# A hybrid decoder layer on one core: the order of the seven block products, accumulating DMAs in place of loads and adds, and stores in two halves

## What is computed

```python
g_gdn, g_moba = split(h @ w_in[:, gates])                 # 2 x 2048 columns
y_gdn, y_moba = oa @ w_out_gdn, ob @ w_out_moba           # 1024 -> 2048 each
merged = sigmoid(g_gdn) * y_gdn + sigmoid(g_moba) * y_moba
x = x + merged @ w_o                                      # 2048 -> 2048
```

## Time and profile before

| | |
|---|---|
| median of 3 runs | 1692.65 us |
| the profiled execution, its own time | 1691.26 us |
| its span, first to last instruction | 1689.6 us |
| granted TensorE clock, mean | 0.987 |
| busy: PE, PEld, DVE, ACT, POOL | 95%, 79%, 67%, 46%, 7% |
| HBM read, written | 199.42 MB, 25.17 MB |
| DMA share, mean rate | 38.4% (SP's queue) and 3.8% (POOL's), 133 GB/s |

### The profile page before, as it was taken

The page is one execution under the profiler, slowest core; times in us unless marked ns, Lnnn a source line. Parts: engine busy times, 40 slices in busy tenths (PEclk is TensorE's granted clock), DMA queues, the critical chain, the costliest instruction groups (busy, mean ns, idle before and its releaser), DMA issues.

```text
span 1689.6 us, 20990 instructions
## 1 busy us (share of the span) xinstructions
PE 1613.4 (95%) x7913; PEld 1332.7 (79%) x7913; DVE 1139.4 (67%) x1367; ACT 780.6 (46%) x1032; POOL 110.3 (7%) x111
## 2 busy tenths in 40 slices
PE   6999999999999999999999998999999887997997
PEld 6888888888888888888888876888888666775786
DVE  5745646646546457456478669687788977798975
ACT  5434434434345344344344344656567544454432
POOL 4100001000001010000011000000000000000000
PEclk9999999999999999999999999999999988999999
DMA  8214222323132142142234264736657466764651
GB/s 253 76 30 127 56 76 81 81 74 87 50 83 79 48 106 81 27 128 56 74 106 131 98 230 145 261 126 223 195 186 244 165 216 215 249 235 151 219 203 64
DMA packets 203644, 225.32 MB, mean 133 GB/s; under 512 B 8035, under 2 KB 140358, under 8 KB 202054
## 3 DMA queue, kind: packets, MB, share of 16 engines
q1 hardware_dynamic: 197126, 199.44, 38.4%
q0 software_dynamic: 6464, 25.17, 3.8%
HBM read 199.42 MB, written 25.17 MB: 133 GB/s over the span
## 4 chain that ended last, share of the span: by engine, by line
PE 82%; DVE 8%; DMA 4%; issue 3%; ACT 2%; SPq 0%; POOL 0%; DVEq 0%; ACTq 0%; POOLq 0%
PE bank L643 14%; PE bank L647 14%; PE bank L645 14%; PE bank L1063 8%; PE bank L1065 8%; PE bank L1067 8%; PE bank L672 6%; DVE ring_lo L1974 2%; PE bank L677 1%; ACT ring_hi L1408 1%; DMA operands<-in_w_in_dram 1%; PE bank L834 1%; DVE e_block L1994 1%; DMA branch_a<-e_block 1%; PE bank L850 1%
## 5 line engine op out<-in xcount | busy, mean ns | idle before, releaser
L643 PE MATMUL bank<-h_hi_r,w_hi 128*128 128x512 f32 x1008 | 421.4, 418 | 0.0
L647 PE MATMUL bank<-h_hi_r,w_raw_r 128*128 128x512 f32 x1008 | 396.8, 394 | 0.0
L645 PE MATMUL bank<-h_lo_r,w_hi 128*128 128x512 f32 x1008 | 394.2, 391 | 0.0
L1408 ACT ACTIVATE ring_hi<-operands 128x1024 fp32r<-128x1024 f32 x224 | 234.6, 1058 | 248.8 <-PE bank L1067 179.6
L1974 DVE TENSOR_TENSOR ring_lo<-operands,ring_hi 128x1024 fp32r<-128x1024 f32 x224 | 271.9, 1221 | 105.0 <-ACT ring_hi L1408 104.2
L647 PEld LDWEIGHTS bank<-h_hi_r,w_raw_r 128*128 128x128 f32 x1008 | 189.1, 188 | 42.9
L645 PEld LDWEIGHTS bank<-h_lo_r,w_hi 128*128 128x128 f32 x1008 | 190.2, 189 | 35.6 <-issue 1.7
L643 PEld LDWEIGHTS bank<-h_hi_r,w_hi 128*128 128x128 f32 x1008 | 190.0, 188 | 35.8 <-issue 1.7
L1063 PE MATMUL bank<-ring_hi,h_hi_r 128*128 128x512 f32 x480 | 192.0, 400 | 13.6 <-DVE ring_lo L1974 6.9
L1065 PE MATMUL bank<-ring_lo,h_hi_r 128*128 128x512 f32 x480 | 190.0, 396 | 0.0
L1539 DVE TENSOR_TENSOR w_raw_r<-w_raw,w_hi 128x2048 fp32r<-128x2048 f32 x64 | 146.7, 2292 | 46.3 <-ACT w_hi L1121 45.1
(11 more groups left out here) (308 smaller groups left out, 2154.1 us busy)
## 6 DMA issues: line engine op xcount, KB each, us to landing
w_raw<-in_w_in_dram SPq DMA_DIRECT2D x64, 1024.0 KB, 6.0
operands<-in_w_in_dram SPq DMA_DIRECT2D x96, 512.0 KB, 5.0
operands<-in_w_o_dram SPq DMA_DIRECT2D x48, 512.0 KB, 6.7
operands<-in_w_out_gdn_dram SPq DMA_DIRECT2D x24, 512.0 KB, 5.0
operands<-in_w_out_moba_dram SPq DMA_DIRECT2D x24, 512.0 KB, 5.8
gates<-e_block POOLq DMA_DIRECT2D x16, 512.0 KB, 5.0
operands<-gates SPq DMA_DIRECT2D x16, 512.0 KB, 6.1
x_tiles<-in_x_dram SPq DMA_DIRECT2D x4, 1024.0 KB, 10.4
```

The source lines that it names most:

```text
L643: pe.matmul(PJ[slot % 2][:], w_hi[slot % 2][:, c], h_hi[:, k, :], start=(k == 0), stop=False, skip_group_check=True)
L645: pe.matmul(PJ[slot % 2][:], w_hi[slot % 2][:, c], h_lo[:, k, :], start=False, stop=False, skip_group_check=True)
L647: mm = pe.matmul(PJ[slot % 2][:], w_lo[slot][:, c], h_hi[:, k, :], start=False, stop=(k == KT - 1), skip_group_check=True)
L1408: act.activation(ring_hi[:, n % RINGS, :], ops[:, SOURCE[p], j, :], ACT.Copy).then_inc(s["op_hi"], 1)
```

## The change

The product order of quads 1 to 9 becomes P11, PS1, PS2, P12, PS4, PS3, P22; quad 0 keeps its order. The roles of the four weight blocks change with it (some sums have the other sign, and the token rows of the stage behind quads 6 and 7 are exchanged), and slots are used otherwise: A holds 11, then T1, then T2; B holds 12, then T3; C holds 21, then T4. In the quads of 4 pieces, T2 = T1 + 22 is made by a DMA on POOL's queue that adds 22 from HBM onto the piece in SBUF, and VectorE makes three sums for each piece; 22 is also loaded plainly once for PS4. In the quads of 2 pieces 22 has two places of its own (A2, A3), each block is loaded once, and VectorE makes four sums. In quads 4 to 7 a fourth `e_block` lies over a free piece of B. The addition of `branch_a` in quads 6 and 7 is an accumulating DMA of POOL, each issued after the one before has landed. The result is filled with x by one 4 MB DMA from HBM to HBM in quad 1, the running values of quads 8 and 9 are copied out by ScalarE, and each result block is added onto the result by two accumulating DMAs of 256 KB. `merged_turn` moves from two to four units after the product's end, `merged_copy` (ACT) from six to eight.

```diff
+FIRST_ORDER = (P11, P12, PS1, PS2, PS4, PS3, P22)
+ORDER = (P11, PS1, PS2, P12, PS4, PS3, P22)
...
+def e_index(q, role):
+    if q < Y0:
+        return (0, 1, 2, 0)[role]
+    return (3, 1, 2, 0)[role] if q < W0 else (2, 1, 0, 2)[role]
...
+TURN, CAUGHT_UP = 4, 8
...
+            return {P11: SLOT_A, PS1: SLOT_A, PS2: SLOT_A, P12: SLOT_C, PS4: SLOT_A, PS3: SLOT_B, P22: SLOT_C}[p], j
...
+            def load_22(q):
 
                 for j in range(ku(q)):
...
+                    if ku(q) == 4:
+                        sp.wait_ge(s["op_lo"], unit(q, PS2, j) + 1)
+                        sp.wait_ge(s["t_formed"], t4_formed(q, j))
+                        load_op(q, SLOT_A, j, 1, 1, j)
                     else:
...
+                        last = 2 + j if ku(q - 1) == 4 else j
+                        sp.wait_ge(s["op_lo"], unit(q - 1, PS4, last) + 1)
+                        sp.wait_ge(s["t_formed"], t3_formed(q - 1, last))
+                        load_op(q, SLOT_A, 2 + j, 1, 1, j)
...
+                if q == 1:
+                    sp.dma_start(outs, xs).then_inc(s["out_filled"], 16)
...
-            load_first(0)
-            load_third(0)
+            load_11(0)
+            load_21(0)
+            load_12(0, range(4))
             sp.wait_ge(s["o_out"], 16 * H)
             load_own(0, sums32(0), s["stage_a"])
-            load_second(0)
...
+            def add_22(q, j):
+
+                pool.wait_ge(s["op_lo"], unit(q, PS1, j) + 1)
+                pool.dma_start(ops[:, SLOT_A, j, :].rearrange("p (k c) -> p k c", k=UK), right(q, 1, 1, j),
+                               accum_op=ALU.add).then_inc(acc[j], 16)
...
+                elif q < W0:
+                    b = 4 * (q - YB) + i
+                    g, k = gate_block(q, i)
+                    pool.wait_ge(s["y_g"], 8 + b + 1)
+                    pool.wait_ge(e_stored[k], stored(q - 2))
+                    if b > 0:
+                        pool.wait_ge(s["part_added"], 16 * b)
+                    pool.dma_start(e, m_dram[q - YB, k], accum_op=ALU.add).then_inc(s["part_added"], 16)
+                else:
+                    pool.wait_ge(s["out_filled"], 16)
+                    for t in range(2):
+                        pool.wait_ge(s["c_add"], 2 * (4 * q + i) + 1 + t)
+                        pool.dma_start(token_block(outs, q, i)[:, t, :], block(q, i)[:, t, :], accum_op=ALU.add)\
+                            .then_inc(e_stored[i], 16)
 
             for q in range(NQ):
...
+                if q == W0:
+                    finish_block(q - 1, 3)
+                if ku(q) == 4:
+                    add_22(q, 0)
+                    add_22(q, 1)
+                if q > 0 and q != W0:
+                    finish_block(q - 1, 3)
+                if ku(q) == 4:
+                    add_22(q, 2)
+                    add_22(q, 3)
+                for i in range(3):
+                    finish_block(q, i)
...
+            def forms(q, n):
+
+                at = n - unit(q)
+                if ku(q) == 4:
+                    late = 1 if q == W0 else 0
+                    if q > 0 and late <= at < 4 + late:
+                        form_t1(q, at - late)
+                    elif 12 <= at < 16:
+                        form_t4(q, at - 12)
+                    elif 17 <= at < 21:
+                        form_t3(q, at - 17)
+                elif at < 2:
+                    form_t1(q, at)
+                elif at < 4:
+                    form_t2(q, at - 2)
+                elif 6 <= at < 8:
+                    form_t4(q, at - 6)
+                elif 8 <= at < 10:
+                    form_t3(q, at - 8)
```

More of the change, by code:

```diff
@@ L638, in _ @@
+            for i in range(4):
+                pool.wait_ge(e_stored[i], stored(NQ - 1))
+        @program.tensor
         def _(pe):
@@ L1403, in op_hi @@
                     act.wait_ge(s["pe_unit"], n - LEAD + 1)
-                if p in (P11, P12, PS4):
-                    act.wait_ge(op_loaded[SOURCE[p]][j], op_loads(q, j, SOURCE[p], (P11, P12, PS4).index(p) // 2))
-                else:
-                    act.wait_ge(s["t_formed"], formed(q, (PS1, PS2, PS3, P22).index(p), j))
-                act.activation(ring_hi[:, n % RINGS, :], ops[:, SOURCE[p], j, :], ACT.Copy).then_inc(s["op_hi"], 1)
+                slot, u = source(q, p, j)
+                if p == P11 or p == P12 or (p == PS4 and ku(q) == 2):
+                    act.wait_ge(op_loaded[slot][u], op_loads(q, u, slot))
+                elif p == PS4:
+                    act.wait_ge(op_loaded[slot][u], op_loads(q, u, slot, 1))
+                elif p == PS1:
+                    act.wait_ge(s["t_formed"], t1_formed(q, j))
+                elif p == PS2 and ku(q) == 4:
+                    act.wait_ge(acc[j], added(q))
+                elif p == PS2:
+                    act.wait_ge(s["t_formed"], t2_formed(q, j))
+                else:
+                    act.wait_ge(s["t_formed"], (t3_formed if p == PS3 else t4_formed)(q, j))
@@ L1507, in _ @@
             copy_out(0, P11)
-            merged_hi_at = {unit(W0 - 1, P12, 1): P11, unit(W0, P11, 3): P12, unit(W0, P12, 2): PS1,
-                            unit(W0, PS1, 2): PS2, unit(W0, PS2, 1): PS4, unit(W0, PS2, 3): PS3,
-                            unit(W0, PS4, 1): P22}
+            merged_hi_at = {unit(W0 - 1, PS4, 1): P11, unit(W0, PS1, 1): PS1, unit(W0, PS2, 0): PS2,
+                            unit(W0, PS2, 1): P12, unit(W0, P12, 0): PS4, unit(W0, P12, 1): PS3,
+                            unit(W0, P12, 3): P22}
             for n in range(8, N_UNITS):
                 op_hi(n)
-                for q in range(W0):
+                for q in range(NQ):
                     for p in (P11, PS1, PS2, PS3):
@@ L1531, in _ @@
                     merged_hi(merged_hi_at[n])
-        @block.vector
+        @program.vector
         def _(dve):
@@ L1973, in op_lo @@
                     dve.wait_ge(s["o_mm"], 4 * H)
[L1974 removed]
+                dve.tensor_tensor(ring_lo[:, n % RINGS, :], operand(q, p, j),
                                   ring_hi[:, n % RINGS, :].bitcast(F32), ALU.subtract).then_inc(s["op_lo"], 1)
             head(last, last - 1)
[L1979 to L1986 removed]
             def block_add(q, i):
[L1990 removed]
+                e, p = block(q, i), BLOCK_PRODUCT[i]
                 dve.wait_ge(s["pe_unit"], ended(q, p))
@@ new lines, in form_t2, with form_t4 @@
+                dve.tensor_tensor(ops[:, SLOT_A, j, :], ops[:, SLOT_A, j, :], ops[:, SLOT_A, 2 + j, :], ALU.add)\
+                    .then_inc(s["t_formed"], 1)
+            def form_t4(q, j):
+                if ku(q) == 4:
+                    dve.wait_ge(acc[j], added(q))
+                else:
+                    dve.wait_ge(s["t_formed"], t2_formed(q, j))
+                dve.wait_ge(s["op_hi"], unit(q, P12, j) + 1)
+                dve.tensor_tensor(ops[:, SLOT_C, j, :], ops[:, SLOT_C, j, :], ops[:, SLOT_A, j, :], ALU.subtract)\
@@ L2156, in _ @@
                 for qb in range(NQ):
-                    for pb in range(NP):
-                        if n == ended(qb, pb) + LEAD - 1:
-                            if qb >= W0 and pb in (P11, PS1, PS2, PS3):
-                                residual(qb, pb)
-                            if pb in BLOCK_PRODUCT:
-                                block_add(qb, BLOCK_PRODUCT.index(pb))
-                forms(q, p, j)
+                    for i in range(4):
+                        if n == ended(qb, BLOCK_PRODUCT[i]) + LEAD - 1:
+                            block_add(qb, i)
+                forms(q, n)
                 if q == 0:
```

469 lines of the change are left out of this document (223 added, 246 removed).

## The result

The changed kernel takes 1649.0 us (median of 4 runs, 1646.6 to 1651.3), the kernel before 1691.7 in the same session: a ratio of 0.9748, 95% interval 0.9731 to 0.9765. The forecast was 1650.

What follows compares the result with a forecast made beforehand. TensorE sets the end; its pauses, 87.6 us, are the pool. 10 + 14.8 + 13.5 + 10 - 4 - 1.3 = 43.0 us off 1691.3 gives 1648.3, median said as 1650; range 1634 to 1684, forecast's own 1638 to 1662.

Steps and rivals of the forecast that it cites:

- Quad 0: Two VectorE load waits and four sums go, two T1 passes lie uncovered: 10 of 20.1 us gained, ends 4.9 and 16.2.
- Quads 4 and 5: Late loads and store waits go, VectorE's work stays: 14.8 us gained, ends 4 and 20.
- the three causes: In quads 4 and 5: late loads of 11, P12 waiting for the previous quad's block_add, the copy after P11 waiting for a store.
- Quads 6 and 7: VectorE falls under 38.3 us in both; 2.6 and 5.5 us stay lost: 13.5 us gained if the new DMA comes in time.
- The charge for the turns: Accumulating DMAs of branch_a take 6 to 7 us from issue to landing; 0.5 us charged at each of 8 turns: minus 4.
- Rival 3: Added DMA late for the turns, 12 us with the wait for the one before: 26 us less gain, 1676 us; chance 0.12.
- Quad 8: VectorE falls to 78.4 us, PS1's left operand is ready 5 us late: 10 us gained, ends 2 and 15.
- T2: T2's additions by DMA land in 7 us, inside the 14.3 us available less the issue: cost 0.
- Rival 1: Accumulating DMAs slow in the engines, above 5 us each TensorE waits in six quads; at 8.0, 1721 us; chance 0.12.
- The 4 MB copy: HBM copy in quad 1 takes at least 11 us, SP's next loads queue behind it: cost 0, up to 5 at half rate.
- The end: The last result block's two accumulating halves land later: +1.3 us, ends -0.3 and +5.
- the forecast's own signs: Quads 0, 4, 5, 6, 7, 8 about 87, 47, 40, 41, 44, 87 us; T2 landing 6 to 7; transpose waits under 1.

Runs made afterwards that it cites:

- the plain DMAs: Against the changed kernel with one semaphore per block for the branch_a additions: T2's additions as plain loads, the result's half blocks as plain stores; 1640.2 us.
- the old order: Against the changed kernel: old order of products in quads 1, 2 and 9, the previous quad's last block stored ahead of the first additions; 1646.1 us.
- three moves: Against the changed kernel with one semaphore per block for the branch_a additions: three instructions moved up in quads 4 and 8; 1639.2 us.

## Why the prediction was right, step by step

- **Quad 0** (10 forecast, 10.2 measured). The upper end, 16.2, counted both load waits in full. The placement is worth 4.2: the forecast's own terms for it were the wait of 6.14 less the two T1 passes, 3.7. The other 6.0 us are the four sums and the wait of 5.19 behind T2 together, 10.1 by the forecast; 2.2 of what is missing is the accumulation, by the plain DMAs. The two were not tried apart.
- **Quads 4 and 5** (14.8 forecast, 15.0 measured). The total is right. Of the three causes the buffer is worth 7.3 us, the early load some 5 (13.1 over quads 4 to 7), and P12's place, to which the forecast gave as much weight, 1 at most in quad 5. What is left in quad 4 is VectorE's work, 46.6 of 47.2 us, as the earlier trace rows had it.
- **Quads 6 and 7** (13.5 forecast before the turns' charge). Without the additions they gain 12.0 and 4.5 us, 16.5 in sum: the forecast expected pauses to stay that went. The reading that VectorE falls under 38.3 us holds in quad 6 (36.4) and, without the chain, in quad 7 (37.1).
- **The charge for the turns** (-4 forecast). This is the term that was mis-sized: 7.8 us in quads 7 and 8 of this profile, of which the landing is 0.8 and the chain on one semaphore 7.0. The landing was forecast well, 6 to 7 us against a median of 7.0 for six of the eight. What the sum left out is the issue: it took each as starting at its multiply. Rival 3 named the wait for the one before, and its mechanism is what happens; it priced it at 26 us, since it let every turn wait.
- **Quad 8** (10 forecast, 7.0 measured; 8.9 without the additions). PS1's left operand is late, as counted (5 us): the first matmul of PS1 stands 5.4 us once the chain is gone. What was not counted is the slow clock after that pause, 2.6 us. What the gain in quad 8 is made of, VectorE's 14.8 us less or the new order, was not tried apart.
- **T2** (0 forecast). The landings took 8.5 us in the median, not 7, and the issue 1.2 instead of 0.53 to 0.73. The longer issue goes with the accumulation and not with a wait for VectorE: the plain ones at the same places took 0.70 to 0.74. It costs nothing in quads 2, 3 and 9 and, against plain loads, 2.2 us in quad 0. In quad 1 it costs 0.7 through the gate store behind it: the forecast had named this wait and, since 5.6 us of it cost nothing before, set it at nothing; at 6.7 it costs. Rival 1 is far off: x was 2.5 us, its point 5. The page "Collectives: The Full Stack" of the Trainium skill (The bandwidth ceiling), by whose figures the forecast estimated 2.7 us a sum, agrees with these 2.5.
- **The 4 MB copy** (0, or 5 at half the rate). It took 16.0 us from issue to landing, and no window shows it: the one long step of quad 1, at unit 35, lies some 15 us before its issue at 1102.6.
- **The end** (-1.3 forecast, -3.6 measured). The landing took 5.5 us against the 3.1 of the earlier trace rows. The "fixed end of the program" was taken as fixed; GpSimd's drain in it was 0.9 us longer.

The error of the sum is 3 us in the profile, and the median is 1 us off; the chain (3.8 more than charged) and the end (2.3 more) are partly made up by quads 6 and 7. That the median came within 1 us of the forecast is in part luck: the chain and the end were off by 3.8 and 2.3 us, quads 6 and 7 by 3.0 the other way, and the chain alone moved by 6 us from one kernel to another. Of the forecast's own signs, the windows of quads 0, 4, 5 and 6 came within 2 us; quads 7 and 8 missed by 3.7 and 3.3, T2 landed in 8.5 us and not 6 to 7, and the transposes waited up to 3.0 us for one addition and not under 1.

The wait in `finish_block` is not there by mistake. The page "DMA: Bandwidth & Descriptors" of the Trainium skill (Why a DMA increments its semaphore by 16 and not by 1) says that with two DMAs in flight on one semaphore the count can be reached before the first has landed, and asks for one semaphore per buffer in flight. No run here shows a wrong count; what these runs show is the price of the other remedy, waiting: 6.1 us between the medians, 3.5 to 4 in two other kernels.

## What to carry to other kernels

When additions or stores go to DMA, read how their completions are counted: DMAs that share a semaphore run one after the other if each wait must be exact, and the landing time, hidden once, is then paid at the pace of the chain. A pause of TensorE is to be priced with the slower work that can follow it, here 2.6 us for a pause of 5.9, and nothing after one of 3.5 in another kernel. A store issued behind slow DMAs on the same queue lands later, and whoever waits for its buffer pays: here 0.7 us in quad 1. At the end of a kernel ask which engine waits for the last landing and what it still has to do after it.

## What the runs showed of the hardware

- An accumulating DMA of 512 KB from HBM into SBUF: 1.2 us to issue on GpSimd (plain 0.72), 8.5 us to land (plain 5.2, both medians), 2.5 us apart when queued (plain 1.26). Issued about 2.7 us apart, in quad 1 of the old order, each landed in 5.9 to 6.0 us. The additions of `branch_a`, of the same size, took 0.87 us to issue.
- A half block of 256 KB added onto HBM lands in 3.5 to 5.5 us at the end of the kernel; a plain one 2.5 to 2.7 us from GpSimd's queue and 2.3 from SP's or ScalarE's, whose issue takes 0.36 and 0.38 us.
- GpSimd's last instruction, a drain, took 4.3 to 6.8 us, began when its waits had ended, and did not wait for stores issued by others: it ended at 1629.0 in a kernel whose last store landed at 1629.2. It was the same to the ns in kernels with the same list of DMAs (5252 in three, 4926 in five). Why two plain halves make it 2.6 us longer than one DMA stays open.
- After a pause of 5.9 us (no addition of branch_a) the granted clock stood at 0.50 for over 5 us, and a unit of 3.6 us took 6.2. Of two pauses of 3.5 us at the same place, one was followed by a clock of 0.50 (changed kernel) and one by 1.00 (three moves).
